# Low-rank projections of the RWKV layer: taken of normalised and shifted tokens, or of unnormalised tokens with mu and mu-1 in the weights

## The reference, cut to what matters

```
xn = rms_norm(x, norm_mix_odd)            # x * gain / sqrt(mean(x^2) + eps)
x_prev = concatenate([shift_prev[:, None], xn[:, :-1]], axis=1)
xx = x_prev - xn
xr, xw, xk, xv, xa, xg = [xn + xx * mu[i] for i in range(6)]
r = xr @ w_rkv[0]; k = xk @ w_rkv[1]; v = xv @ w_rkv[2]
w_log = -softplus(-(w0 + tanh(xw @ w1) @ w2)) - 0.5
a = sigmoid(a0 + (xa @ a1) @ a2)
g = sigmoid(xg @ g1) @ g2
```

## Time and profile before

| | us |
|---|---|
| median of three runs | 1580.28 (1578.26 to 1580.69) |
| the profiled execution's own time | 1587.68 |
| its span in the profile | 1585.8 |
| PE busy in it | 1498.8 (95%), 17804 matmul records |
| DVE busy | 442.2 (28%) |
| ACT busy | 220.9 (14%) |
| POOL busy | 164.7 (10%) |

### The profile page before, as it was taken

The page is one execution under the profiler, slowest core; times in us unless marked ns, Lnnn a source line. Parts: engine busy times, 40 slices in busy tenths (PEclk is TensorE's granted clock), DMA queues, the critical chain, the costliest instruction groups (busy, mean ns, idle before and its releaser), DMA issues.

```text
span 1585.8 us, 39125 instructions
## 1 busy us (share of the span) xinstructions
PE 1498.8 (95%) x17804; PEld 974.7 (61%) x17804; DVE 442.2 (28%) x962; ACT 220.9 (14%) x479; POOL 164.7 (10%) x208
## 2 busy tenths in 40 slices
PE   6999989999995998999899999999999999999985
PEld 4767877777773777889764555545454555545432
DVE  1289321111006456353631011211111011211123
ACT  3134120000002511131330000000000000000001
POOL 3127200000000224105200000000000000000100
PEclk9899999999997999998899999999999999999997
DMA  9636034353531430032489999999999999999992
GB/s 286 189 126 163 14 108 157 109 159 112 180 107 53 134 93 2 3 56 56 100 308 362 414 413 413 374 415 375 413 387 395 414 371 413 370 415 374 403 399 73
DMA packets 187551, 384.86 MB, mean 243 GB/s; under 512 B 42463, under 2 KB 125631, under 8 KB 187258
## 3 DMA queue, kind: packets, MB, share of 16 engines
q1 hardware_dynamic: 180352, 365.84, 62.6%
q0 software_dynamic: 3616, 12.85, 2.1%
q10 hardware_dynamic: 3418, 3.68, 0.7%
HBM read 375.59 MB, written 6.73 MB: 241 GB/s over the span
## 4 chain that ended last, share of the span: by engine, by line
PE 85%; DVE 9%; DMA 3%; ACT 1%; issue 1%; SPq 0%; DVEq 0%; POOL 0%; ACTq 0%; POOLq 0%
PE bk L1589 26%; PE bk L1606 14%; PE bk L1076 11%; PE bk L761 8%; PE bk L1089 5%; PE bk L1510 2%; PE bk L1557 2%; PE bk L1169 2%; PE bk L991 2%; DMA got<-expert_rows,spot_now 2%; DMA ring<-in_w_in_even 1%; PE bk L1103 1%; DVE left L2158 1%; DVE tops L2156 1%; PE bk L1113 1%
## 5 line engine op out<-in xcount | busy, mean ns | idle before, releaser
L1589 PE MATMUL bk<-part,xe 128*32 128x352 f32 x6144 | 459.1, 460 | 2.3 <-DVE xe L2580 2.3
L1589 PEld LDWEIGHTS bk<-part,xe 128*32 128x32 f32 x6144 | 207.1, 110 | 249.0 <-issue 246.5
L1606 PE MATMUL bk<-part,hidT 128*32 128x256 f32 x4224 | 234.7, 382 | 5.7 <-DVE hidT L2619 5.7
L1606 PEld LDWEIGHTS bk<-part,hidT 128*32 128x32 f32 x4224 | 141.5, 111 | 97.1 <-DVE hidT L2619 8.9
L1076 PE MATMUL bk<-xn,ring 128*128 128x288 f32 x704 | 173.8, 411 | 3.2 <-DMA ring<-in_ffn_up 3.2
L2615 DVE TENSOR_TENSOR hp<-sg,bk 128x352 f32<-128x352 f32 x48 | 37.5, 781 | 470.8 <-PE bk L1589 470.8
L1076 PEld LDWEIGHTS bk<-xn,ring 128*128 128x128 f32 x704 | 135.4, 192 | 41.2 <-issue 3.4
L761 PE MATMUL bk<-xg,ring 128*128 128x288 f32 x336 | 90.4, 429 | 9.9 <-DMA ring<-in_w_in_even 8.3
L761 PE MATMUL bk<-mx,ring 128*128 128x288 f32 x384 | 96.2, 409 | 0.0
L1089 PE MATMUL bk<-hid,ring 128*128 128x288 f32 x352 | 85.5, 406 | 0.0
L761 PEld LDWEIGHTS bk<-xg,ring 128*128 128x128 f32 x336 | 66.5, 201 | 30.3 <-issue 9.1
(11 more groups left out here) (512 smaller groups left out, 1368.6 us busy)
## 6 DMA issues: line engine op xcount, KB each, us to landing
part<-in_moe_gate SPq DMA_DIRECT2D x136, 704.0 KB, 7.3
part<-in_moe_up SPq DMA_DIRECT2D x136, 704.0 KB
part<-in_moe_down SPq DMA_DIRECT2D x128, 704.0 KB, 8.3
ring<-in_rwkv_w_rkv SPq DMA_DIRECT2D x24, 512.0 KB, 3.9
ring<-in_ffn_gate SPq DMA_DIRECT2D x22, 512.0 KB, 5.6
ring<-in_ffn_up SPq DMA_DIRECT2D x22, 512.0 KB, 6.7
ring<-in_ffn_down SPq DMA_DIRECT2D x22, 512.0 KB, 4.2
ring<-in_w_in_even SPq DMA_DIRECT2D x16, 512.0 KB, 5.9
```

The costliest lines, as they stand in the source:

```text
L1589: last = mm(banks[g][32 * c:32 * c + 32, 0:FQ], xe[:, k, 32 * g:32 * g + 32], parts[ph % 3][:, FH * k + FQ * c:FH * k + FQ * c + FQ], star ...
L1606: last = mm(down_bk[g // 2][32 * q:32 * q + 32, 256 * (g % 2):256 * (g % 2) + 256], hidT[:, half, g, 32 * m:32 * m + 32], parts[ph % 3][:, ...
```

## The change

The gain is put on as soon as a chunk of the residual is there: `xg2 = xT * gain`, without the norm, four chunks after each half of the down projection. Eight more columns of `xg2` hold the samples' shift state, so it has TX = 296 columns. While the second half of the down projection runs, DVE multiplies `w1`, `a1` and `g1` by mu into `wS`, and beside each puts the same times mu-1 (the scaled weights less the weights). PE multiplies both by `xg2`: for w and a the two of 64 columns stand side by side in one matmul of 128, for g they are two matmuls, the second into bank 0. The first four chunks of w and a come ahead of the sum of squares, those of g behind it, then the last four chunks of all three. DVE then puts in the shift and the norm: the product with mu times `rs`, one token to the right, less the product with mu-1 times `rs`; ACT takes it from there as before. The tokens themselves are normalised in one instruction over all 2304 elements after that, then `xx` (now one subtraction over prompt and samples with the samples' first tokens overwritten), then the mixed tokens of k and r; those of w, a and g are not made any more. ACT squares each chunk as its residual is there, the sum of squares goes to bank 4. The ring slots of `w1`, `a1` and `g1` are freed by DVE's scaling. POOL waits for the normalised tokens ahead of `e_last`, and for `xg2` alone ahead of `rmask`. Left out below is the placing of the new tiles in memory and the renaming of semaphores.

```diff
-        add_cols(n + "1", I[w1_][0], [(0, I[w1_].shape[2])], lh_mm, i + 1)
+        add_cols(n + "1", I[w1_][0], [(0, I[w1_].shape[2])], scaled_then_mix, KC * (i + 1))
...
-        pe.wait_ge(down_ok, 8)
-        rms_pe(pe, 1, sq2)
         h_in = [(0, HD), (1, HD), (2, P)]
-        for i, r in h_in:
-            pe.wait_ge(mix_ok, KC * (i + 1))
-            w = weights(pe, n0 + i)[:, 0:KC * r].rearrange("p (k n) -> p k n", k=KC)
-            for k in range(KC):
-                last = mm(bk[5 + i][0:r, 0:T], w[:, k], mx[:, i % 2, k], start=k == 0, stop=k == KC - 1)
-            last.then_inc(lh_mm, 1)
+        a_bank, b_bank = (5, 6, 7), 0
+
+        def down_products(i, ks):
+            pe.wait_ge(scaled_then_mix, KC * (i + 1))
+            for k in ks:
+                pe.wait_ge(xn_ok, KC + k + 1)
+                at = LORA_COL[i]
+                last = mm(bk[a_bank[i]][:, 0:TX], wS[:, k, at:at + P], xg2[:, k], start=k == 0, stop=k == KC - 1)
+                if i == 2:
+                    last = mm(bk[b_bank][:, 0:T], wS[:, k, at + P:at + 2 * P], xg2[:, k, 0:T], start=k == 0, stop=k == KC - 1)
+            return last
+
+        pe.wait_ge(down_ok, 5)
+        early, late = range(KC // 2), range(KC // 2, KC)
+        down_products(0, early)
+        down_products(1, early)
+        rms_pe(pe, 1, sq2, 4)
+        down_products(2, early)
+        for i in range(3):
+            down_products(i, late).then_inc(lh_mm, 1)
...
-        act.wait_ge(down_ok, 8)
-        rms_act(act, 1, xT, sq2)
+        for c in range(KC):
+            act.wait_ge(down_ok, c + 1)
+            nc.scalar.activation(sq2[:, c], xT[:, c], ACT.Square).then_inc(sq_ok, 1)
+        act.wait_ge(ms_ok, 2)
+        nc.scalar.activation(rs[:], ms[:], ACT.Sqrt).then_inc(sd_ok, 1)
         for i, (r, f) in enumerate(((HD, ACT.Tanh), (HD, ACT.Copy), (P, ACT.Sigmoid))):
-            act.wait_ge(lh_mm, i + 1)
-            nc.scalar.activation(lh[0:r, i], bk[5 + i][0:r, 0:T], f).then_inc(lh_ok, 1)
+            act.wait_ge(low_then_xx, i + 1)
+            nc.scalar.activation(lh[0:r, i], lhp[0:r, i], f).then_inc(lh_ok, 1)
...
+        def gained(c):
+            g_ = VEC["norm_mix_odd"] + c
+            V.tensor_scalar(xg2[:, c, 0:T], xT[:, c], vecT[:, g_:g_ + 1], None, ALU.mult).then_inc(xn_ok, 1)
+
+        V.memset(prev[:, :, 0:1], 0.0)
         for half in range(2):
             dve.wait_ge(down_mm, (half + 1) * (FC // 2))
             for c in range(4):
                 o = (4, 5, 6, 7)[c] if half == 0 else c
                 V.tensor_tensor(xT[:, 4 * half + c], xT[:, 4 * half + c], bk[o][:, 0:T], ALU.add).then_inc(down_ok, 1)
+            dve.wait_ge(down_ok, 4 * half + 4)
+            if half == 0:
+                V.tensor_copy(xg2[:, :, T:TX], shiftT)
+            for c in range(4 * half, 4 * half + 4):
+                gained(c)
+            if half == 0:
+                dve.wait_ge(out_done, 16 * OUT_0)
+                for i, m in enumerate((1, 4, 5)):
+                    r, at, v_ = LORA_RANK[i], LORA_COL[i], VEC["mu"] + KC * m
+                    w = weights(dve, index_of("wag"[i] + "1"))[:, 0:KC * r].rearrange("p (k n) -> p k n", k=KC)
+                    mu = vecT[:, v_:v_ + KC].unsqueeze(2).broadcast_to([P, KC, r])
+                    link(V.tensor_tensor(wS[:, :, at:at + r], w, mu, ALU.mult))
+                    V.tensor_tensor(wS[:, :, at + r:at + 2 * r], wS[:, :, at:at + r], w, ALU.subtract).then_inc(scaled_then_mix, KC)
...
-        dve.wait_ge(down_ok, 8)
-        rms_dve(dve, link, 1, xT, VEC["norm_mix_odd"], xn2)
-        dve.wait_ge(xn_ok, 2 * KC)
+        rms_factor(dve, link, 1, 4)
+        for i, r in enumerate(LORA_RANK):
+            dve.wait_ge(lh_mm, i + 1)
+            a = slice(0, r)
+            b, b_bank = (a, 0) if i == 2 else (slice(r, 2 * r), 5 + i)
+            V.tensor_tensor(prev[a, i, 1:T], bk[5 + i][a, 0:T - 1], rs[a, 0:T - 1], ALU.mult)
+            link(V.tensor_tensor(lhp[a, i], bk[b_bank][b, 0:T], rs[b], ALU.mult))
+            link(V.tensor_copy(prev[a, i, TP:T].rearrange("p (b t) -> p b t", b=NB)[:, :, 0], bk[5 + i][a, T:TX]))
+            V.tensor_tensor(lhp[a, i], prev[a, i], lhp[a, i], ALU.subtract).then_inc(low_then_xx, 1)
+        V.tensor_tensor(xn2[:], xg2[:, :, 0:T], rs[:].unsqueeze(1).broadcast_to([P, KC, T]), ALU.mult).then_inc(low_then_xx, 1)
+        dve.wait_ge(low_then_xx, 4)
...
-        V.tensor_tensor(xx[:, :, 1:TP], xn2[:, :, 0:TP - 1], xn2[:, :, 1:TP], ALU.subtract)
         V.tensor_scalar(xx[:, :, 0:1], xn2[:, :, 0:1], -1.0, None, ALU.mult)
-        for c in range(KC):
-            V.tensor_tensor(ds_[:, c, :, 1:TS], xs[:, c, :, 0:TS - 1], xs[:, c, :, 1:TS], ALU.subtract)
-        V.tensor_tensor(ds_[:, :, :, 0], shiftT, xs[:, :, :, 0], ALU.subtract).then_inc(xx_ok, 1)
-        dve.wait_ge(xx_ok, 1)
+        link(V.tensor_tensor(xx[:, :, 1:T], xn2[:, :, 0:T - 1], xn2[:, :, 1:T], ALU.subtract))
+        V.tensor_tensor(ds_[:, :, :, 0], shiftT, xs[:, :, :, 0], ALU.subtract).then_inc(low_then_xx, 1)
+        dve.wait_ge(low_then_xx, 5)
...
-        for i, m in enumerate((1, 4, 5, 2, 0)):
-            if i >= 2:
-                dve.wait_ge(lh_mm, i - 1)
-            mixed(i, m)
+        mixed(3, 2)
+        mixed(4, 0)
...
+        pool.wait_ge(low_then_xx, 4)
         G_.tensor_copy(e_last[:, :, 0], xn2[:, :, TP - 1]).then_inc(el_ok, 1)
```

More of the change, by code:

```diff
@@ L278, in build @@
     mx = sbt("mx", [P, 2, KC, T])
-    sq2 = sbt("sq2", [P, KC, T], at=starts["mx"])
+    wS = sbt("wS", [P, KC, 4 * P], at=starts["mx"])
     BK = sbt("BK", [P, KC, 2 * T])
@@ L284, in build @@
     sqk = sbt("sqk", [P, KC, T], at=starts["BK"])
+    sq2 = sbt("sq2", [P, KC, T], at=starts["BK"])
+    TX = T + NB
+    xg2 = sbt("xg2", [P, KC, TX], at=starts["t1"])
+    prev = sbt("prev", [P, 3, T], at=starts["t1"] + 4 * KC * TX)
+    lhp = sbt("lhp", [P, 3, T], at=starts["t1"] + 4 * KC * TX + 12 * T)
+    assert ends["lhp"] <= ends["vT"]
+    LORA_RANK = (HD, HD, P)
+    LORA_COL = (0, P, 2 * P)
     lh = sbt("lh", [P, 3, T], at=starts["BK"] + 9216)
@@ L426, in build @@
     gu_mm, silu_ok, hid_ok, down_mm, down_ok = sem("gu_mm"), sem("silu_ok"), sem("hid_ok"), sem("down_mm"), sem("down_ok")
-    xx_ok, mix_ok, lh_mm, lh_ok = (sem(n) for n in ("xx_ok", "mix_ok", "lh_mm", "lh_ok"))
+    low_then_xx, scaled_then_mix, lh_mm, lh_ok = (sem(n) for n in ("low_then_xx", "scaled_then_mix", "lh_mm", "lh_ok"))
     el_ok, mask_ok, cum_ok, e_ok, kf_ok = (sem(n) for n in ("el_ok", "mask_ok", "cum_ok", "e_ok", "kf_ok"))
@@ L451, in build @@
     plan = Plan()
+    index_of = lambda name: [item[0] for item in plan.items].index(name)
     small_at = {n: i + 1 for i, n in enumerate(("rs", "iw", "iw_s", "isum", "quota", "heads", "out"))}
@@ L649, in rms_factor @@
         link(nc.vector.reciprocal(rs[:], rs[:]))
-    def rms_dve(dve, link, n, src, gain, dst):
-        rms_factor(dve, link, n)
-        for c in range(KC):
-            nc.vector.scalar_tensor_tensor(dst[:, c], src[:, c], vecT[:, gain + c:gain + c + 1], rs[:],
-                                           ALU.mult, ALU.mult).then_inc(xn_ok, 1)
     block = ctx.enter_context(nc.Block())
@@ L2241, in _ @@
             V.tensor_tensor(hid[:, f], sg[:, f % 2], us[:, f % 2], ALU.mult).then_inc(hid_ok, 1)
+        shiftT = vecT[:, VEC["state_shift"]:VEC["state_shift"] + 64].rearrange("p (b c) -> p c b", b=NB)
+        def gained(c):
+            g_ = VEC["norm_mix_odd"] + c
+            V.tensor_scalar(xg2[:, c, 0:T], xT[:, c], vecT[:, g_:g_ + 1], None, ALU.mult).then_inc(xn_ok, 1)
+        V.memset(prev[:, :, 0:1], 0.0)
         for half in range(2):
@@ L2253, in _ @@
+        V.tensor_tensor(xn2[:], xg2[:, :, 0:T], rs[:].unsqueeze(1).broadcast_to([P, KC, T]), ALU.mult).then_inc(low_then_xx, 1)
+        dve.wait_ge(low_then_xx, 4)
         xs = xn2[:, :, TP:T].rearrange("p c (b t) -> p c b t", b=NB)
         ds_ = xx[:, :, TP:T].rearrange("p c (b t) -> p c b t", b=NB)
-        shiftT = vecT[:, VEC["state_shift"]:VEC["state_shift"] + 64].rearrange("p (b c) -> p c b", b=NB)
-        V.tensor_tensor(xx[:, :, 1:TP], xn2[:, :, 0:TP - 1], xn2[:, :, 1:TP], ALU.subtract)
@@ L2267, in mixed @@
                 V.scalar_tensor_tensor(mx[:, i % 2, c], xx[:, c], vecT[:, v_:v_ + 1], xn2[:, c],
-                                       ALU.mult, ALU.add).then_inc(mix_ok, 1)
-        for i, m in enumerate((1, 4, 5, 2, 0)):
-            if i >= 2:
-                dve.wait_ge(lh_mm, i - 1)
-            mixed(i, m)
+                                       ALU.mult, ALU.add).then_inc(scaled_then_mix, 1)
+        mixed(3, 2)
+        mixed(4, 0)
         V.tensor_scalar(omk[:], vecT[:, ka:ka + KC], -1.0, 1.0, ALU.mult, ALU.add)
```

## The result

The changed kernel takes 1565.14 us (median of four runs, 1562.23 to 1569.18) where the kernel before took 1580.49 beside it (1578.26 to 1582.18): ratio 0.9905, 95% interval 0.9877 to 0.9932. Timed again later, on six runs against eleven, it was 1568.92 against 1582.52, ratio 0.9917 (0.9897 to 0.9936). The forecast was 1565.3 us, 15.0 less than before, in a range of 1562.8 to 1569.5. It is faster, by 13.6 to 15.4 us as the two pairs of medians have it.

What follows compares the result with a forecast made beforehand. The bound was taken to be the unoverlapped chain of waits from down projection to k jobs. With its terms summed, k jobs start at 512.93 instead of 527.89; 1580.28 - 15.0 = 1565.3 us, range 1562.8 to 1569.5.

Steps and rivals of the forecast that it cites:

- What bounds it: Last down matmul to first k job: 48.27 us of waits through DVE, ACT and PE, with nothing overlapping.
- Start: PE's first low-rank product waits only for the second half's first residual, and starts at 480.08 us.
- PE's part: Products of w, a and g plus sum of squares on PE: 19.73 us, of which 15.85 are products.
- Norm: Root and reciprocal after the sum of squares: 3.04 us, ready 2.9 us before w's products, so hidden.
- Put-in shift and norm: DVE's set after each projection: 1.5 us, bounds 1.3 to 2.0; hidden for w and a, exposed for g.
- Second products: PE's 24 products after g's projection: start 499.81, fifth waits for a bank until 502.3, end at 512.05 us.
- DVE's slack: DVE's work after g: k's mixes 2.4 us early for the k jobs, 2.1 us to spare at the fifth.
- Costed at nothing: DVE's scaling of w, a and g weights, about 5 us, covered by the second half of the down projection.
- Clock: TensorE from down projection through products: clock 1.00 throughout; one fall and rise costs 2.4 us.
- Rival C: TensorE falls to 1.2 GHz in the new products and keeps it; time 1585.1 us; chance 0.03 for slower.
- Downstream: The k jobs and all behind them move as one block, so the 15.0 us reach the end.
- rival B: Experts' weight stream near the DMA limit bounds the end, so the time stays 1580 us; chance 0.02.

Runs made afterwards that it cites:

- experiment 6: Changed kernel with one more DVE instruction of 2304 elements ahead of the normalised tokens; first residual after last down matmul to first k job 34.42 us, against 34.00.
- Experiment 3: Changed kernel with the sum of squares first and all low-rank products held until the reciprocal; first residual after last down matmul to first k job 39.16 us, against 34.00.
- Experiment 5: Changed kernel with ACT taking the first four second products out of PSUM before g's sigmoid; first residual to first k job 33.40 us, against 34.00.
- 7: Changed kernel with three more DVE instructions of 2304 elements ahead of the normalised tokens; first residual to first k job 39.60 us, against 34.00.
- Experiment 8: Changed kernel with ACT's other order and POOL's spread copy ahead of its wait for normalised tokens; median 1567.99 us (ratio 0.9933 to kernel before), later 1567.03 (0.9896).
- experiment 2: Kernel before with 26 idle matmuls behind the sum of squares; first residual after last down matmul to first k job 45.83 us, against 48.25 and 48.06.
- 4: Changed kernel with the scaling of weights moved behind the second half's residuals; first residual after last down matmul to first k job 39.45 us, against 34.00.

## Why the prediction was right

- *What bounds it.* As said: the chain's 14 us of DVE and ACT are gone and PE has no gap over 0.55 us.
- *Start.* Forecast 0.46 us behind the last down matmul, measured 0.53 (473.16 to 473.69). Sums of squares behind w and a, no wait on squares.
- *PE's part.* Forecast 19.73 us, measured 20.01 (473.69 to 493.70). Nearly all of the 0.3 is in the first 16 records, 4.25 us where 16 x 0.2493 is 3.99. It is what a start behind a wait costs: the k jobs of experiment 6, behind 0.41 us of wait at the full clock, take 0.24 more too. The forecast had no term for it.
- *Norm.* Forecast hidden by 2.9 us. DVE took up w's products 3.08 us after the reciprocal was done. Experiment 3 shows the cover to be worth 5.2 us, since it also keeps the clock.
- *Put-in shift and norm.* Forecast 1.5, measured 1.53 us.
- *Second products.* This term was off: forecast 12.24 us with its wait, measured 12.62. It was mis-added: by its own rows (four products at 0.50 us from 499.81 on) the fifth would have come at 501.8 and not at 502.2, so it waits 0.5 us for the bank, and the other 20 at the pace of 12.03 / 24 end at 512.33, which makes 12.52. As written PE waits 0.1 us and then runs at 0.4875 us a product. It waited 0.34 and then needed 10.16 us for 20, 0.51 each, behind ACT. Experiment 5 gives 12.03.
- *DVE's slack.* The forecast had two places: 2.4 us in front of the first k job, and 2.1 us, the smaller, in front of the fifth. Experiments 6 and 7 measure 2.1 at the first place. At the second the changed kernel has 2.4 us: ACT's third copy ended at 520.26, and the fifth k job was due at 507.19 + 64 x 0.2425 = 522.71. So the bound lay in the other place, 0.3 us lower than forecast, and the same number is chance. `cumx` was there 44.7 us after the last down matmul, forecast 44.1. The 0.66 us that POOL took out of k's and r's mixes are in it. The Trainium skill ("GPSIMD Engine Reference", section 1, Specifications) has GpSimd in contention with VectorE instructions of two SBUF inputs. Experiment 8 agrees, with 0.66 us lost to a copy of 1.11. That is within the 1.03 us that the forecast allowed and put into the slack and not into the sum.
- *Costed at nothing.* The scaling took 5.2 us and was done 23.8 us early. Without its cover it costs 5.45, mostly as forecast, 1.7 of it through the clock, which the forecast had not put there.
- *Clock.* Forecast 2.4 us gained by not falling; experiment 2 has 2.2 to 2.4. Rival C did not come: 1.00 throughout.
- *Downstream.* The rest took 1057.6 to 1058.3 us in the changed kernel and 1057.7 to 1057.9 before: it moved as one block, and rival B falls.

The sum was 15.0 where the stretch gave 14.25: 0.07 too many in the start, 0.28 in PE's part, 0.38 in the second products. The median came within 0.2 us of the forecast, which is closer than the terms deserve: 0.75 us of them were too many, and the medians spread by more than that between timings.

## What to carry to other kernels

A linear step between a normalisation and a narrow projection can be put behind the projection when the weights can be scaled under other work; then the products themselves cover the reduction and the root. Count what it costs on the engine that becomes the bound (here eight more matmuls, 3.9 us) and how much slack the freed engine has behind it (2.1 us), for both are found in the trace before. Read such a gain from the stretch between two fixed instructions, since whole spans differed by 3 us and more with nothing changed.

## What the runs showed of the hardware

- Gaps of 1.9 and 2.24 us without matmuls left TensorE at its full clock (experiment 2); gaps of 3.18 and 4.3 us were each followed by 3.4 us at 1.2 GHz, which began only when PE was at work again (3.5 and 5.1 us behind its last matmul, experiments 3 and 4) and cost 1.7 us. In the 14.5 us gap of the kernel before the grant fell while PE stood still, 2.4 us behind its last matmul. A wait on PE can so cost more than it lasts.
- A group of matmuls that starts behind a wait of PE takes about 0.25 us more than its records at their pace, also at the full clock: 4.25 us for 3.99 behind 0.53 us, 35.16 for 34.92 behind 0.41 us (changed kernel, experiment 6).
- The third group of k, r and v jobs, 48 records behind narrow matmuls with 16 rows, took 11.84 us in one profile of the kernel before and 13.53 in the next, and 13.52 in the changed kernel. In the changed kernel's profile the granted clock was at its lower level there for 3.4 us, with PE busy all the time; in the first profile of the kernel before it was 1.00 throughout:

```profile
557.00:562.00 5.00, 5.00 (x21) 3.33 (x19) 3.16 (x7) 0.40 (x1) 0.00 (x0) 1.00 0.40 116
562.00:567.00 5.00, 5.00 (x15) 3.68 (x15) 4.94 (x5) 0.00 (x0) 0.00 (x0) 0.66 0.01 3
567.00:572.00 5.00, 5.00 (x23) 3.90 (x22) 3.26 (x3) 0.71 (x2) 0.00 (x0) 1.00 0.36 105
```

  These are windows of the changed kernel, columns as in the earlier trace rows. This is part of the spread of the rest. From the start of the 16-row matmuls (L1140, in the changed kernel L1155) to the end of these 48 records it was 15.9 us in three of the thirteen profiles, 17.6 in four and 19.2 in six. The lowered clock comes in both kernels; but all six of 19.2 are of the changed kernel and its variants, and with three profiles of the kernel before it is not shown whether the change makes them more likely.
- POOL's copy waits for DVE's long subtraction and DVE does not wait for POOL: a copy of 64 columns took 2.61 us beside it in the changed kernel and 0.32 just behind it, while the subtraction took 2.55 us for 2296 columns there and 2.28 for 2040 in the kernel before.
